# Layer norm and root mean square norms with sums by chunk and a diagonal matrix for the scaling

## The chip, the core and the metric
The kernel runs on one core of a Trainium2 chip. The metric is the device time of one execution in microseconds (us); a lower time is better. TensorE (PE) multiplies, VectorE (DVE), ScalarE (ACT) and GpSimd (POOL) work on tiles of 128 partitions, and SyncE (SP) issues the weight loads.

## What is computed
A transformer block with mixture of experts, followed by two further layers and a final norm, on 256 tokens of width 2048, all in float32:

```
x = _layer_norm(ALPHA * x + mix, ln1_w, ln1_b)
moe = _hier_moe(x, ...)                       # 32 experts, D_EXPERT 512
ple = sigmoid(x @ w_pg) * (p @ w_ple)
x = _layer_norm(ALPHA * x + moe + ple, ln2_w, ln2_b)      # "last layer norm"

def rmsnorm(x, g):                            # EPS = 1e-6
    return x * rsqrt(mean(x * x, -1) + EPS) * g

# even layer: chunked attention and an S5 state space model
x = x + concat(o_a, o_b) @ w_out_even,   inputs from rmsnorm(x, norm_even_g) @ w_in_even
# odd layer: forgetting attention, 16 heads of 128
x = x + o @ w_out_odd,                   inputs from rmsnorm(x, norm_odd_g) @ w_in_odd
return rmsnorm(x, final_norm_g)
```

The change is about the second layer norm and the three calls of rmsnorm.

## The kernel before
The whole program is written out by hand, one instruction stream for each engine, with semaphores between them. The 256 tokens are two row blocks b of 128 partitions, so x is a tile [128, 2, 2048] in SBUF. Each engine's helper issues an instruction and makes it wait for the one before it on its engine (`ordered`); so nearly all instructions of an engine carry one of a few helper lines: L137 is a PE product, L143 a PE transpose, L254 and L256 an ACT activation without and with a bias tile, L283 DVE tensor_tensor, L288 and L290 tensor_scalar, L294 scalar_tensor_tensor, L298 a reduction, L306 and L310 the statistics of a batch norm and their aggregation, L275 a reciprocal.

PSUM is a ring of four banks of 1024 columns (`Ring`, `take`, `free`). The weights come through a stream of six raw buffers; in the fp32r parts (the odd layer, the output projections) ACT copies a piece to its high half and DVE subtracts for the low half. `ahead_of(key)` does these halvings up to two pieces ahead of where PE is. In the even layer's input products the weights are used as plain float32, without halving. The experts' weights are streamed by SP (`quarter`) through ten slots of 1 MB, each reused when the product that read it is done (`used.w`).

The stretches that matter here, in the order of the program:

- **End of the experts.** PE scatters the last expert's result back to the tokens in four groups of products (row block b, column set c); DVE adds each to x (`scattered`, L1738 ff.). Then every engine branches over a rarely needed part (`beyond`) and the engines meet (`meet(7)`, `meet(8)`).
- **Second layer norm** (`layer_norm("l2", None)`). For each row block DVE takes statistics of four chunks, aggregates, adds 1e-5; ACT takes the square root; DVE the reciprocal, a subtract-and-multiply over 2048 columns, a product with ln2_w and a sum with ln2_b. Both vectors are loaded by POOL after `meet(7)`, spread over all partitions.
- **Norm of the even layer** (`rms("r1", ...)`). For each row block DVE squares (2048 columns), reduces, scales; ACT square root; DVE reciprocal and one scalar_tensor_tensor that multiplies x by the reciprocal and by the norm's weights into hne. Then PE transposes hne in four banks of eight 128x128 blocks, and ACT and DVE copy two banks each to hTe, in which channels lie on partitions. Products of the even layer start when all of hTe is there. On DVE the S5 setup follows, on POOL the tables of phases made from it.
- **Between even and odd layer.** `add_scaled("ev.out", 1.0)` adds the output product to x chunk by chunk as PE finishes each of four; then `meet(12)`, `rms("r2", ...)`, with norm_odd_g loaded by POOL after the meeting; PE transposes; ACT copies each bank to the high half of hT_ and DVE subtracts for the low half. The odd layer begins with the forget gate's rows (`od.f`).
- **End.** `add_scaled("od.out", 1.0)`, `meet(14)`, `rms("r3", ...)`, and ACT sends the result [256, 2048] with one transfer.

## Time and profile before

| | us |
|---|---|
| median of three runs | 3428.41 (3428.26 to 3434.42) |
| the profiled execution's own time | 3427.37 |
| its span in the profile | 3425.7 |
| PE busy | 3067.3 (90%) |
| DVE busy | 1568.2 (46%) |
| ACT busy | 826.3 (24%) |
| POOL busy | 266.5 (8%) |

### The profile page before, as it was taken

How to read it: one execution, taken by the hardware profiler on the slowest of the kernel's cores; microseconds unless marked ns; L12 is line 12 of the kernel's file. 1: busy time of each engine (PE TensorE's matmuls, PEld its weight loads, DVE VectorE, ACT ScalarE, POOL GpSimd, SP SyncE). 2: the span in 40 equal slices, each digit the busy share in tenths (PEclk: the TensorE clock that was granted, in tenths of full speed). 3: DMA queues.
4: the chain of work that ended last, by engine and by line, in shares of the span. 5: the costliest groups of instructions: out<-in, count | busy, mean ns of one | idle time of the engine just before them, and what ended most of it. 6: DMA issues, size and time to landing. Idle time of an engine off the chain costs nothing.

```text
span 3425.7 us, 42547 instructions
## 1 busy us (share of the span) xinstructions
PE 3067.3 (90%) x18244; PEld 2201.7 (64%) x18244; DVE 1568.2 (46%) x1856; ACT 826.3 (24%) x911; POOL 266.5 (8%) x247
## 2 busy tenths in 40 slices
PE   8978999889995899999999999679998788999987
PEld 6767777889975653333333333268777678987875
DVE  4454543564544622222222222439885445444544
ACT  3342222434431321111100110000001333443332
POOL 2042111000000000000000000044320000000000
PEclk9999988889996899999999999889999999998898
DMA  6543211336563569999999999733443365885443
GB/s 210 149 134 100 76 57 57 99 107 186 176 199 97 170 241 425 425 425 425 425 425 425 425 425 425 301 111 111 123 123 109 113 180 130 181 182 123 97 137 129
DMA packets 213809, 724.18 MB, mean 211 GB/s; under 512 B 16074, under 2 KB 18506, under 8 KB 162540
## 3 DMA queue, kind: packets, MB, share of 16 engines
q1 hardware_dynamic: 209340, 698.03, 58.7%
q0 software_dynamic: 3728, 19.15, 1.6%
q8 instruction: 146, 2.39, 0.3%
q10 hardware_dynamic: 544, 4.19, 0.3%
q14 instruction: 51, 0.42, 0.0%
HBM read 719.21 MB, written 2.10 MB: 211 GB/s over the span
## 4 chain that ended last, share of the span: by engine, by line
PE 68%; DMA 14%; DVE 12%; ACT 3%; issue 1%; POOL 1%; DVEq 0%; ACTq 0%; POOLq 0%
PE psum L137 67%; DMA t<-in_w_up 13%; DVE t L283 9%; ACT t L254 3%; PE psum L143 1%; DVE t L294 1%; DVE t L298 1%; DMA t<-in_ln_b 0%; ACT t L256 0%; POOL t L328 0%; POOL t L323 0%; DMA t<-in_r_k 0%; DMA t<-in_norm_odd_g 0%; DVE t L288 0%; DVE t L306 0%
## 5 line engine op out<-in xcount | busy, mean ns | idle before, releaser
L137 PE MATMUL psum<-t,t 128*128 128x256 f32 (+8 forms) x17134 | 2955.1, 382 | 216.1 <-DVE t L283 121.9
L137 PEld LDWEIGHTS psum<-t,t 128*128 128x128 f32 (+5 forms) x17134 | 2096.5, 178 | 1041.8 <-issue 607.8
L283 DVE TENSOR_TENSOR t<-t,t 128x1024 fp32r<-128x1024 f32 (+6 forms) x650 | 801.4, 1233 | 631.4 <-ACT t L254 595.7
L254 ACT ACTIVATE t<-t 128x1024 fp32r<-128x1024 f32 (+5 forms) x523 | 528.7, 1011 | 1036.9 <-PE psum L137 705.6
L283 DVE TENSOR_TENSOR t<-t,psum 128x1024 f32<-128x1024 f32 (+3 forms) x265 | 246.3, 929 | 760.0 <-PE psum L137 484.1
L254 ACT ACTIVATE t<-psum 128x1024 f32<-128x1024 f32 (+5 forms) x276 | 211.7, 767 | 1454.7 <-PE psum L137 1327.6
L328 POOL TENSOR_TENSOR t<-t,t 128x1024 f32<-128x1024 f32 (+9 forms) x125 | 210.3, 1682 | 572.0 <-DVE t L283 258.2
L143 PE MATMUL psum<-t,t 128*128 128x128 f32 (+1 forms) x598 | 96.9, 309 | 107.2 <-DVE t L294 62.8
L283 DVE TENSOR_TENSOR t<-psum,t 128x1024 f32<-128x1024 f32 (+5 forms) x129 | 105.1, 815 | 144.7 <-PE psum L137 125.8
L143 PEld LDWEIGHTS psum<-t,t 128*128 128x128 f32 (+1 forms) x598 | 77.5, 159 | 142.7 <-issue 89.2
L269 DVE COPY t<-psum 128x256 f32<-128x256 f32 (+5 forms) x85 | 50.4, 593 | 150.5 <-PE psum L143 97.3
L83 POOL DMA_DIRECT2D t<-in_ln_w x2 | 1.1, 554 | 1214.8 <-DVE t L283 1121.6
L298 DVE TENSOR_REDUCE t<-t 128x4 f32<-128x1024 f32 (+8 forms) x67 | 61.6, 919 | 3.0 <-ACT t L256 0.7
L254 ACT ACT_TABLE_LOAD x35 | 44.9, 1283 | 44.5 <-DVE t L290 21.5
L137 PE MATMUL psum<-t 64*64 64x64 f32 (+2 forms) x512 | 41.6, 282 | 10.3 <-ACT t L254 5.8
L302 DVE TENSOR_TENSOR_SCAN t<-t,t 128x256 f32<-128x256 f32 (+1 forms) x65 | 44.7, 688 | 2.2
L83 POOL DMA_DIRECT2D t<-in_final_norm_g x1 | 0.6, 569 | 552.7 <-DVE t L294 552.7
L137 PEld LDWEIGHTS psum<-t 64*64 64x64 f32 (+2 forms) x512 | 34.0, 184 | 14.2 <-ACT t L254 7.6
L290 DVE TENSOR_SCALAR t<-t,t,t 128x64 f32<-128x64 f32 x128 | 40.2, 314 | 4.6
L283 DVE TENSOR_TENSOR t<-t 128x2048 f32<-128x2048 f32 (+8 forms) x46 | 35.6, 773 | 1.6
L256 ACT ACTIVATE t<-psum,t 128x256 f32<-128x256 f32 (+1 forms) x56 | 24.9, 444 | 24.0 <-PE psum L137 22.4
L269 DVE COPY t<-t 64x64 f32<-64x64 f32 x64 | 29.2, 456 | 2.2
(65 smaller groups left out, 225.5 us busy)
## 6 DMA issues: line engine op xcount, KB each, us to landing
t<-in_w_gate SPq DMA_DIRECT2D x128, 1024.0 KB, 17.0
t<-in_w_up SPq DMA_DIRECT2D x128, 1024.0 KB, 19.0
t<-in_w_down SPq DMA_DIRECT2D x128, 1024.0 KB, 18.0
t<-in_w_in SPq DMA_DIRECT2D x160, 512.0 KB, 3.6
t<-in_w_in_odd SPq DMA_DIRECT2D x128, 512.0 KB, 5.5
t<-in_w_in_even SPq DMA_DIRECT2D x96, 512.0 KB, 3.8
t<-in_w_out SPq DMA_DIRECT2D x32, 512.0 KB, 3.7
t<-in_w_pg SPq DMA_DIRECT2D x32, 512.0 KB, 4.4
```

The costliest lines, as they stand in the source:

```text
L83: self.e.dma_start(out, in_).then_inc(self.counts.sem(name), 16)
L137: ins = self.e.matmul(o, l, r, start=start, stop=stop, skip_group_check=True)
L143: ins = self.e.transpose(o, i, self.ident[0:k, 0:k])
L254: self.put(self.e.activation(o, i, f, scale=scale), event)
L256: self.put(self.e.activation(o, i, f, bias=bias, scale=scale), event)
L269: self.put(self.e.tensor_copy(o, i), event)
L283: self.put(self.e.tensor_tensor(o, a, b, op), event)
L290: self.put(self.e.tensor_scalar(o, a, s1, s2, o1, o2), event)
L294: self.put(self.e.scalar_tensor_tensor(out=o, in0=a, scalar=s, in1=b, op0=o1, op1=o2), event)
L298: self.put(self.e.tensor_reduce(o, i, AX.X, op), event)
L302: self.put(self.e.tensor_tensor_scan(o, d0, d1, init, o0, o1), event)
L328: self.put(self.e.tensor_tensor(o, a, b, op), event)
```

## The change
The second layer norm and the three root mean square norms are rewritten:

- **Sums chunk by chunk.** Where DVE adds a chunk to x (the last expert's scatter, the even and the odd output product), it takes the batch norm statistics of that chunk at once. The mean square is the variance plus the squared mean. Squares and reductions over 2048 columns are gone.
- **Layer norm 2 and norm r1 in one pass** (`second_norm`): for each 512 columns two scalar_tensor_tensor, `(x - mean) * ln2_w` and `x * inv + ln2_b`, and new statistics. ln2_w and ln2_b are loaded through SP's expert slots, behind the last expert's weights.
- **Scaling as a product.** The reciprocal of each token goes on the diagonal of a 128x128 matrix (`diag[b]`, the identity times a column), and a float32 product of each block of x with it replaces both the scaling and the transpose. The weights of the norm (`gains`) now lie along partitions and are applied when the bank is read: in the even layer by 24 ACT activations of 128 columns with a scale tile and a bias tile (a column of zeros) and one DVE operation of 1024 columns, in the odd layer by 16 ACT activations (high half) and 16 scalar_tensor_tensor on DVE (low half), each of 256 columns.
- **Four parts.** The last norm is scaled by chunks of 512 columns and ACT sends each of four parts when both row blocks are there.
- The meetings 8, 9, 12, 13 and 14 are gone, some tiles have other places, and POOL's selector for the odd layer and the load of final_norm_g wait for earlier events.

```diff
@@ def vector_program
+            def second_norm():
+                aggregate()
+                v.ts(spread, var, 1e-5, None, ALU.add, event=("l2.var",))
+                v.wait_ge(("l2.std",))
+                v.rcp(inv, stdev)
+                first = place["w_down", 31, 3] + 1
+                v.wait_ge(("landed.w", first), ("landed.w", first + 1))
+                for b in range(2):
+                    for ci in range(4):
+                        xc, cs = x[:, b, 512 * ci:512 * ci + 512], slice(512 * ci, 512 * ci + 512)
+                        v.stt(xc, xc, mv[:, b, 0:1], l2w[:, cs], ALU.subtract, ALU.mult)
+                        v.stt(xc, xc, inv[:, b:b + 1], l2b[:, cs], ALU.mult, ALU.add)
+                        sums(v, 0, ci, b, 512 * ci)
+                    v.bn_aggr(m2, lst[:, 0:24])
...
+                    v.ts(s2, s2, 1e-6, None, ALU.add, event=("r1.var", b))
+                    v.wait_ge(("r1.std", b))
+                    v.rcp(i2, d2)
+                    v.ts(diag[b], ident, i2, None, ALU.mult, event=("r1.diag", b))
@@ def scattered
+                            if ex == 31:
+                                for h in range(2):
+                                    sums(v, 24 * b, 2 * c + h, b, 1024 * h + 512 * c)
@@ def tensor_program
-            turn_into("ev.T", hne, 2048, ("ev.h",))
+            for b in range(2):
+                for h in range(2):
+                    ps = pe.take("ev.T", b, h)
+                    pe.wait_ge(("r1.diag", b))
+                    for k in range(8):
+                        pe.mm(ps[:, 128 * k:128 * k + 128], x[:, b, 1024 * h + 128 * k:1024 * h + 128 * k + 128], diag[b],
+                              True, True, event=("ev.T", b, h) if k == 7 else None)
@@ def scalar_program
-            for j in (0, 2):
-                a.wait_ge(("ev.T", j))
-                a.copy(hTe[:, 4 * j:4 * j + 4, :].rearrange("p k (b t) -> p b k t", b=2),
-                       a.bank("ev.T", j).rearrange("p (b k t) -> p b k t", b=2, k=4), event=("ev.hT", "act"))
+            std("l2", lst[:, 54:56], lst[:, 52:54])
+            for b in range(2):
+                std("r1", lst[:, 61:62], lst[:, 60:61], b)
+                for h in range(b, 2):
+                    a.wait_ge(("ev.T", b, h), ("landed.gains",))
+                    for k in range(8):
+                        a.activation(hTe[:, 8 * h + k, 128 * b:128 * b + 128],
+                                     a.bank("ev.T", b, h)[:, 128 * k:128 * k + 128], ACT.Identity, bias=cols[:, 2:3],
+                                     scale=gains[0][:, 8 * h + k:8 * h + k + 1], event=("ev.hT", "act"))
...
-            a.load(("landed.out",), [(out[0].rearrange("(b p) d -> p b d", p=128), hn)])
+            for ci in range(4):
+                cs = slice(512 * ci, 512 * ci + 512)
+                a.wait_ge(("out.h", ci))
+                a.load(("landed.out", ci), [(whole[:, :, cs], hn[:, :, cs])])
@@ def pool_program
-            g.load(("landed.l2",), [(lnw, along("ln2_w")), (lnb, along("ln2_b"))])
-            g.load(("landed.r1",), [(rwe, along("norm_even_g_2"))])
```

How it moves instructions. On DVE, behind the last expert's sums, before (t_76 is x, t_72 the small sums, t_113 and t_114 ln2, t_175 hne; from the second row block's statistics on):

```order
L306 BN_STATS t_72<-t_76 128x6 x4
L310 BN_AGGR t_72<-t_72 128x2
L288 TENSOR_SCALAR t_72<-t_72 128x1
L275 RECIPROCAL t_72<-t_72 128x1
L290 TENSOR_SCALAR t_76<-t_76,t_72 128x2048
L283 TENSOR_TENSOR t_76<-t_76,t_113 128x2048
L283 TENSOR_TENSOR t_76<-t_76,t_114 128x2048
L283 TENSOR_TENSOR t_175<-t_76 128x2048
L298 TENSOR_REDUCE t_177<-t_175 128x1
L290 TENSOR_SCALAR t_177<-t_177 128x1
L275 RECIPROCAL t_177<-t_177 128x1
L294 SCALAR_TENSOR_TENSOR t_175<-t_76,t_177,t_176 128x2048
```

and now (t_134 and t_135 are ln2, t_61 the identity, t_62 the diagonal of row block 0; "..." stands for three more chunks):

```order
L306 BN_STATS t_72<-t_76 128x6 x8
L2150 UNCONDITIONAL_BRANCH
L310 BN_AGGR t_72<-t_72 128x2 x2
L288 TENSOR_SCALAR t_72<-t_72 128x2
L275 RECIPROCAL t_72<-t_72 128x2
L294 SCALAR_TENSOR_TENSOR t_76<-t_76,t_72,t_134 128x512
L294 SCALAR_TENSOR_TENSOR t_76<-t_76,t_72,t_135 128x512
L306 BN_STATS t_72<-t_76 128x6
...
L294 SCALAR_TENSOR_TENSOR t_72<-t_72 128x1
L288 TENSOR_SCALAR t_72<-t_72 128x1
L275 RECIPROCAL t_72<-t_72 128x1
L288 TENSOR_SCALAR t_62<-t_61,t_72 128x128
```

The statistics stand ahead of the branch, the norm's scaling over 2048 columns is gone, and a small diagonal ends each row block. On ACT at the same place, before (t_72 and t_177 the square roots, t_168 hTe, the copies of whole banks):

```order
L2485 UNCONDITIONAL_BRANCH
L254 ACT_TABLE_LOAD
L254 ACTIVATE t_72<-t_72 128x1 x2
L254 ACTIVATE t_177<-t_177 128x1 x2
L254 ACTIVATE t_168<-psum 128x2x4x128 x2
L254 ACT_TABLE_LOAD
L254 ACTIVATE t_204<-t_203 128x32
```

and now (t_167 is hTe, t_111 the gains, t_70 the column of zeros):

```order
L2548 UNCONDITIONAL_BRANCH
L254 ACT_TABLE_LOAD
L254 ACTIVATE t_72<-t_72 128x2
L254 ACTIVATE t_72<-t_72 128x1
L256 ACTIVATE t_167<-psum,t_70,t_111 128x128 x16
L254 ACTIVATE t_72<-t_72 128x1
L256 ACTIVATE t_167<-psum,t_70,t_111 128x128 x8
L254 ACT_TABLE_LOAD
L254 ACTIVATE t_184<-t_183 128x32
```

The second row block's square root now stands behind the 16 reads of the first block. On DVE between the even and the odd layer, before (t_165 is the scaled x, t_78 and t_77 the low and high half):

```order
L294 SCALAR_TENSOR_TENSOR t_76<-t_76,psum 128x2x512
L283 TENSOR_TENSOR t_165<-t_76 128x2048
L298 TENSOR_REDUCE t_167<-t_165 128x1
L290 TENSOR_SCALAR t_167<-t_167 128x1
L275 RECIPROCAL t_167<-t_167 128x1
L294 SCALAR_TENSOR_TENSOR t_165<-t_76,t_167,t_166 128x2048
L283 TENSOR_TENSOR t_165<-t_76 128x2048
L298 TENSOR_REDUCE t_167<-t_165 128x1
L290 TENSOR_SCALAR t_167<-t_167 128x1
L275 RECIPROCAL t_167<-t_167 128x1
L294 SCALAR_TENSOR_TENSOR t_165<-t_76,t_167,t_166 128x2048
L283 TENSOR_TENSOR t_78<-psum,t_77 128x2x4x128 x4
```

and now (t_62 and t_63 are the diagonals):

```order
L283 TENSOR_TENSOR t_76<-t_76,psum 128x2x512
L306 BN_STATS t_72<-t_76 128x6 x2
L310 BN_AGGR t_72<-t_72 128x2 x2
L283 TENSOR_TENSOR t_72<-t_72 128x2 x2
L288 TENSOR_SCALAR t_72<-t_72 128x2
L275 RECIPROCAL t_72<-t_72 128x2
L288 TENSOR_SCALAR t_62<-t_61,t_72 128x128
L288 TENSOR_SCALAR t_63<-t_61,t_72 128x128
L294 SCALAR_TENSOR_TENSOR t_78<-psum,t_112,t_77 128x256 x16
```

Ten operations of the norm, six of them over 2048 columns, became ten small ones, and the four low halves of 1024 columns became 16 of 256.

## Rows read from the trace of the kernel before

**Rows 1.** Chain of waits, two joints: start us, us, engine and tile, count.
```profile
2243.84 6.42 PE psum L143 x32
2251.63 55.49 PE psum L137 x256
...
2836.27 3.66 PE psum L143 x16
2844.95 5.64 PE psum L137 x48
```

**Rows 2.** Timeline of DVE at the three joints; in brackets idle before, and releaser.
```profile
2197.96 5.20 DVE L283 TENSOR_TENSOR t<-t,psum 128x1024 f32<-128x1024 f32 x4 [7.93 <-PE psum L137]
2206.20 2.88 DVE L306 BATCH_NORM_STATS2 t<-t 128x6 f32<-128x512 f32 x4 [3.04 <-issue]
...
2211.27 0.16 DVE L275 RECIPROCAL t<-t 128x1 f32<-128x1 f32 x1 [1.71 <-ACT t L254]
...
2815.62 1.22 DVE L294 SCALAR_TENSOR_TENSOR t<-t,psum 128x1024 f32<-128x1024 f32 x1 [0.46 <-PE psum L137]
...
3400.84 1.22 DVE L294 SCALAR_TENSOR_TENSOR t<-t,psum 128x1024 f32<-128x1024 f32 x1 [6.00 <-PE psum L137]
```

**Rows 3.** Groups of ACT by form: line, shapes, count | busy us, mean ns | idle.
```profile
L254 ACT ACTIVATE t<-psum 128x256 f32<-128x256 f32 x80 | 30.7, 384 | 145.0 <-PE psum L137 140.0 <-PE psum L143 0.7
...
L256 ACT ACTIVATE t<-psum,t 128x256 f32<-128x256 f32 x40 | 19.0, 475 | 16.0 <-PE psum L137 14.9
...
L256 ACT ACTIVATE t<-psum,t 128x128 f32<-128x128 f32 x16 | 5.9, 368 | 8.0 <-PE psum L137 7.5
L256 ACT ACTIVATE t<-t,t 128x256 f32<-128x256 f32 x8 | 4.8, 600 | 0.3
```

**Rows 4.** Timeline of PE in the mLSTM part; two records are one float32 product.
```profile
661.07 0.47 PE L137 MATMUL psum<-t 128*128 128x128 f32 x2
661.37 0.28 PE L137 MATMUL psum<-t,t 128*128 128x1 f32 x2
...
664.24 0.77 PE L137 MATMUL psum<-t 128*128 128x128 f32 x2
664.81 0.42 PE L137 MATMUL psum<-t,t 128*128 128x1 f32 x2
```

**Rows 5.** Groups of DVE by form, columns as in rows 3.
```profile
L294 DVE SCALAR_TENSOR_TENSOR t<-t,t,t 128x2048 f32<-128x2048 f32 x6 | 14.1, 2352 | 0.2
...
L306 DVE BATCH_NORM_STATS2 t<-t 128x6 f32<-128x512 f32 x16 | 11.1, 694 | 3.6 <-issue 3.0
...
L294 DVE SCALAR_TENSOR_TENSOR t<-t,t,t 128x255 f32<-128x255 f32 x8 | 3.9, 484 | 0.3
...
L294 DVE SCALAR_TENSOR_TENSOR t<-t,t,psum 128x256 f32<-128x256 f32 x8 | 3.8, 480 | 26.5 <-PE psum L137 26.5
```

**Rows 6.** Stretches: us, PE, PEld, DVE, ACT, POOL busy, clock, DMA, GB/s.
```profile
2816.00:2822.00 6.00, 0.00 (x0) 0.00 (x0) 5.57 (x4) 0.17 (x1) 0.58 (x1) 0.79 1.01 160
2838.00:2840.00 2.00, 2.00 (x11) 2.00 (x11) 0.70 (x1) 1.07 (x2) 0.00 (x0) 0.51 0.00 0
2840.00:2842.00 2.00, 1.75 (x16) 1.52 (x14) 1.52 (x2) 1.91 (x2) 0.00 (x0) 1.00 0.00 0
2842.00:2845.00 3.00, 0.05 (x1) 0.06 (x2) 2.68 (x3) 1.19 (x3) 0.00 (x0) 1.00 0.00 0
3130.00:3135.00 5.00, 5.00 (x13) 2.59 (x11) 0.67 (x2) 0.00 (x0) 0.00 (x0) 0.50 0.01 3
3308.00:3312.00 4.00, 3.32 (x8) 2.64 (x9) 1.85 (x2) 0.52 (x1) 0.00 (x0) 0.50 0.18 55
```

**Rows 7.** ACT's output issue, in its timeline.
```profile
3418.91 0.40 ACTq L83 DMA_DIRECT2D out<-t  x1
```

**Rows 8.** DMA issues: KB each, median us to landing.
```profile
t<-in_w_out_odd SPq DMA_DIRECT2D x32, 512.0 KB, 3.6
...
out<-t ACTq DMA_DIRECT2D x1, 2048.0 KB, 6.3
```

More of the change, by code:

```diff
@@ L444, in build @@
         bg = alloc(32)
+        gains = [at(invm_at + 768 + 16 * k, 16) for k in range(2)]
+        diag = [shiftd, carry]
         assert top[0] <= invm_at + 896
@@ new lines, in add_and_sum @@
+            def add_and_sum(key):
+                for ci in range(4):
+                    v.ahead_of(key, ci)
+                    cs = slice(512 * ci, 512 * ci + 512)
+                    v.wait_ge((key, ci))
+                    v.tt(x[:, :, cs], x[:, :, cs], half(v.bank(key, ci)), ALU.add)
+                    v.free(key, ci)
+                    for b in range(2):
+                        sums(v, 24 * b, ci, b, 512 * ci)
+            mv = lst[:, 48:52].rearrange("p (b k) -> p b k", b=2)
+            mean, var = mv[:, :, 0], mv[:, :, 1]
@@ L2117, in vector_program @@
[L2117 to L2122 removed]
+            root_mean_square("r2")
+            for b in range(2):
+                v.ts(diag[b], ident, inv[:, b:b + 1], None, ALU.mult, event=("r2.diag", b))
+            for j in range(4):
+                v.ahead_of("od.T", j)
+                ps = v.bank("od.T", j).rearrange("p (b k t) -> p b k t", b=2, k=4)
+                dh, dl = [z[:, 4 * j:4 * j + 4, :].rearrange("p k (b t) -> p b k t", b=2) for z in hT_]
+                v.wait_ge(("od.Th", j))
+                for k in range(4):
+                    v.stt(dl[:, :, k, :], ps[:, :, k, :], gains[1][:, 4 * j + k:4 * j + k + 1],
+                          dh[:, :, k, :].bitcast(F32), ALU.mult, ALU.subtract, event=("od.hT",))
+                v.free("od.T", j)
@@ L2125, in scalar_program @@
+            odd()
+            add_and_sum("od.out")
+            root_mean_square("r3")
+            v.wait_ge(("landed.r3",))
+            for ci in range(4):
+                cs = slice(512 * ci, 512 * ci + 512)
+                for b in range(2):
+                    v.stt(hn[:, b, cs], x[:, b, cs], inv[:, b:b + 1], rwt[:, cs], ALU.mult, ALU.mult,
+                          event=("out.h", ci) if b else None)
         def scalar_program(e):
```

140 lines of the change are left out of this document (67 added, 73 removed).

## The prediction

> **What bounds the kernel now.** I read the chain of waits first, then the timelines of the engines at its joints, then the clock by stretch. The program is TensorE (PE) work end to end, except at three joints where one x must be complete before anything goes on. At the first, the last expert's sums end on VectorE (DVE) at 2203.16 [rows 2]; PE stands still until 2243.84, then transposes for 6.42 us and starts the even layer at 2251.63 [rows 1]. At the second, between the even and the odd layer, the last product's sum ends at 2816.84 [rows 2], transposes start at 2836.27 and the odd layer at 2844.95 [rows 1]. At the third, x is complete at 3402.06 [rows 2] and the span ends at 3425.7: 6.8 us after the single output transfer is issued at 3418.91 [rows 7]. Between the joints PE is the chain, so a gain at a joint is handed on whole unless something else is late there. I lay out the changed joints instruction by instruction and subtract.
>
> **Prices.** DVE: statistics of 128x512 0.694, with the 0.03 to the next 0.72. The three-operand scaling of 512 columns lies on the line between 0.484 (255 columns) and 2.352 (2048): 0.484 + 257 x 0.00104 = 0.75, 0.785 with its gap [rows 5]. From the end of the variance to the instruction after the reciprocal: 1.71 idle (the square-root table is loaded in it) + 0.16 + 0.04 = 1.9 [rows 2]; with the table in place, 0.47. ScalarE (ACT): a PSUM read of 128x256 is 0.384 plain and 0.475 with a bias from a tile, so an operand from a tile costs 0.09; the new reads have two, so 0.566 for 256 columns and 0.368 + 0.09 = 0.46 for 128; pitches 0.60 and 0.49. Bounds: the one-operand rows, and 0.60 + 0.03 of the two-operand form from SBUF [rows 3]. PE: no row has these products alone; the nearest is a float32 product of 128 columns in the mLSTM part: 0.30 from start to start at full clock (661.07 to 661.37), 0.57 at half (664.24 to 664.81) [rows 4]. A bank of eight is 2.4 or 4.6. Half of 0.57 could be hidden at best, for the transposes it replaces take 0.23 at the low clock (16 in 3.66) [rows 1].
>
> **First joint.** Eight statistics go in between the four last sums: 2197.96 + 4 x 1.30 + 8 x 0.72 = 2208.95. Queued behind them are the weight loads of the even layer and the S5 loads on the POOL queue, 6 us later than before; nothing wants them before 2245, and three transfers of 1 MB have left that queue. The two ln2 rows ride on the SP queue behind the last experts, when DVE is 30 us from wanting them: free. The 3.04 us of issue time after the branch stay [rows 2]: 2212.0. Two aggregations and one small operation 0.77, square root and reciprocal 1.9: 2214.65. Per row block b: 4 x (2 x 0.785 + 0.72) = 9.17, aggregation and two small ones 0.73, reciprocal 0.47, diagonal 0.26: 10.6. So diagonal 0 is there at 2225.25, variance 1 at 2235.15. PE has been idle and is at half clock: bank (0,0) ends at 2229.8, (0,1) at 2232.2. ACT drains each with eight reads, 3.9 us: 2233.8 and 2237.7. Here a **new wait** appears: the square root for block 1 stands behind these 16 reads on ACT, so it comes at 2237.9 and not at 2235.3, and diagonal 1 at 2238.45. PE: 4.6 + 2.4 gives 2245.4; ACT's last eight reads end at 2249.4. The even layer starts there, against 2251.63: **2.2** earned of 8 us that DVE gains. DVE's own half (one 1.22 us operation) and the S5 setup behind it are done in that cover; the setup starts 2 to 4 us earlier as well, since its memsets no longer come after the last copy, so POOL's phase tables stay ahead.
>
> **Clock at the restart.** PE then has stood for 4.0 us. The granted clock after work that ended at 2815.56 had fallen within the stretch to 2822 (mean 0.79, so some 2.5 of its 6 us at half); the odd output projection, after a pause, began at half clock (0.50 over 3308 to 3312); but after 3.19 us from 2841.76 it was still 1.00 [rows 6]. From a cold start it is back after about 4 us (transposes from 2836.27, 0.51 up to 2840, 1.00 after) [rows 1, 6]. I take cold: half of 4 us, **2.0** lost. First joint net 0.2.
>
> **Second joint.** Sum ends 2816.84; two statistics 1.45 (the six others run while PE still multiplies: DVE has over 9 of 22 us free per chunk), aggregations 0.58, three small 0.56, square root and reciprocal 1.9, two diagonals 0.52: 2821.9. The 2816.88 to 2836.12 of squares, reductions, a load of norm_odd_g and scalings are gone. PE cold again: first bank 2826.5, the others by 2833.7. ACT is the slow one: 16 reads x 0.60 = 9.5, to 2836.05; the last four low halves on DVE (0.480 + 0.03 each [rows 5]) to 2838.2. The odd layer starts 6.6 us earlier; its restart after 4.6 us of standing costs 2.0: net **4.6**. The forget-gate rows and the split weights behind it keep their order.
>
> **Third joint.** Sum 3402.06, two statistics, aggregations, three small, 1.9: 3406.6. Eight scalings x 0.785: 3412.9. The last quarter, 512 KB, takes 3.6 like a load of 512 KB, not the 6.3 of the whole, and 0.5 stay behind it (3418.91 + 6.3 against the span) [rows 7, 8]: 3417.0, **8.7** earned. Bounds for the quarter: 1.6 (a quarter of 6.3) and 6.3.
>
> Sum: 0.2 + 4.6 + 8.7 = 13.5. The profiled execution took 3427.37 (span 3425.7), so 3413.9; the median of the runs, 3428.41, is 1.0 above it: **3414.9 us**.
>
> **A rule of the skill, weighed.** The window 2838 to 2840 is at 0.51 and 2840 to 2842 at 1.00 with only transposes running [rows 6]. The Trainium skill ("TensorE: Matmul & The Clock Gate", Part 4: PE-mode transpose) says that transposes do not count as PE work for the clock, so that they run low; real products would then bring the clock up where transposes did not, and the change would gain both restarts (the result of rival 1). By that rule 3410.9, by the rows 3414.9: the trace contradicts it here.
>
> **Rivals.** (1) The clock stays up over both restarts: pauses of 4.0 and 4.6 are little longer than the 3.19 that did no harm. 13.5 + 4.0 = 17.5: **3410.9**. (2) Products as slow as at half clock throughout. In the mLSTM part the clock fell during just such products, with PE busy: 0.30 apiece at 661.07, 0.57 at 664.24 [rows 4]. Then block 1 ends at 2247.6 and the even layer starts at 2251.6 (0, less 2 for the restart); od.T banks end at 2840.2, last low half at 2844.7 (0.2, less 2). Net 8.7 - 3.8 = 4.9: **3423.5**. (3) The four parts do not do what they say: a quarter takes as long as the whole, so the third joint earns 6.0: **3417.6**. (4) The drains are as cheap as one-operand reads (0.40 and 0.50), or the quarter lands in 1.6, together with (1): about **3406**. (5) **Slower.** The restarted layers stay at half clock far beyond 4 us. It happens: PE was busy in all of 3130 to 3135 at 0.50 [rows 6], some 30 us in all, in the odd layer's scores. Were the first 30 us of both restarted layers like that, 2 x 15 are lost: 17.5 - 30 = -12.5, **3440.9**. It decides from 35 us of added half clock on. Against it: the layer's first products are the same as before, and they ran at full clock from a restart within 2 us of transposes.
>
> **Chances.** Forecast 0.50; (1) 0.20; (2) 0.13; (3) 0.08; (4) 0.05; (5) 0.04. The unknown prices (reads 0.50 to 0.63 for 0.60, products, quarter) move the forecast by about 4 either way. Range 3407 to 3424: it leaves out (4), (5) and half of (2) with thin tails. A measurement here tells 0.2%, 6.9 us, from no change. Faster by more: the forecast but for a tail, (1), (3), (4): 0.81. Within: (2) and the tail: 0.15. Slower: 0.04.
>
> **What would show it.** Right: the even layer's first product some 2 us earlier with ACT's reads just before it, a reciprocal that waits on ACT for over 2 us in the second block, reads of 0.46 and 0.57, products of 0.57 then 0.30, a low clock in the first 4 us of each layer, the odd layer 4 to 7 us earlier relative to its last sum, and the end about 15 us after the last sum instead of 24. Wrong: reads above 0.63, a DVE wait for the ln2 rows, a pause on POOL's phase tables, or half clock without idle time behind it.

## The result and the profile after

The changed kernel takes 3409.79 us (median of five runs, 3405.9 to 3410.73) against 3428.26 (five runs, 3423.31 to 3434.42): ratio 0.9945, interval 0.9931 to 0.996. The forecast was 3414.9 with a range of 3407 to 3424. The profiled execution took 3409.92 us, its span is 3407.6 (3425.7 before); the mean granted clock is 0.945 (0.941).

**First joint.** Timeline of DVE of the changed kernel (start us, us, engine, line, operation, out<-in, shapes, count; in brackets idle time before, and what ended it), the rows that answer to [rows 2]:

```profile
2199.47 1.22 DVE L283 TENSOR_TENSOR t<-t,psum 128x1024 f32<-128x1024 f32 x1 [7.93 <-PE psum L137]
...
2215.68 0.56 DVE L310 BATCH_NORM_AGGREGATE t<-t 128x2 f32<-128x24 f32 x2 [5.18 <-issue]
...
2218.17 0.17 DVE L275 RECIPROCAL t<-t 128x2 f32<-128x2 f32 x1 [1.71 <-ACT t L254]
...
2241.30 0.16 DVE L275 RECIPROCAL t<-t 128x1 f32<-128x1 f32 x1 [2.19 <-ACT t L254]
```

ACT, same kernel and place:

```profile
2233.09 7.88 ACT L256 ACTIVATE t<-psum,t,t 128x128 f32<-128x128 f32 x16 [4.46 <-PE psum L137]
...
2247.51 3.90 ACT L256 ACTIVATE t<-psum,t,t 128x128 f32<-128x128 f32 x8 [6.25 <-PE psum L137]
```

and PE (two records are one float32 product):

```profile
2229.30 6.71 PE L137 MATMUL psum<-t,t 128*128 128x128 f32 x32 [24.64 <-DVE t L288]
2241.84 5.63 PE L137 MATMUL psum<-t,t 128*128 128x128 f32 x32 [5.83 <-DVE t L288]
2251.46 4.76 PE L137 MATMUL psum<-t,t 128*128 128x256 f32 x13 [3.99 <-ACT t L256]
```

The new wait is there: the second row block's square root stands behind 16 reads on ACT, ends at 2241.26, and DVE's reciprocal has waited 2.19 for it. A read takes 0.49 and a product 0.42 (6.71 for 16; PE was at half clock for 6 of these 6.7 us). PE starts the even layer after 3.99 us of standing, on ACT's last reads. The issue time after the branch is 5.18, not the 3.04 of [rows 2].

**Clock at the restarts.** Stretches of the changed kernel (us, busy time of PE, PE weight loads, DVE, ACT, POOL, granted clock, DMA share, GB/s), answering to [rows 6]. In both joints PE runs at half clock for 3.5 to 5 us once it has restarted:

```profile
2252.00:2254.00 2.00, 2.00 (x7) 1.68 (x6) 0.60 (x4) 1.66 (x4) 0.00 (x0) 0.61 0.00 0
...
2256.00:2258.00 2.00, 2.00 (x11) 1.75 (x10) 1.32 (x7) 0.42 (x2) 0.00 (x0) 1.00 0.08 7
...
2838.00:2840.00 2.00, 1.78 (x9) 1.25 (x10) 1.29 (x2) 0.52 (x1) 0.00 (x0) 0.50 0.00 0
...
2842.00:2844.00 2.00, 2.00 (x16) 1.50 (x14) 0.00 (x0) 0.00 (x0) 0.00 (x0) 0.76 0.66 136
```

Its chain of waits, answering to [rows 1]: the even layer's first 256 records take 57.21 us instead of 55.49, and the forget gate's rows (od.f) 7.85 instead of 5.64.

```profile
2251.46 57.21 PE psum L137 x256
...
2838.22 7.85 PE psum L137 x48
```

**Second joint.** DVE and ACT of the changed kernel, in order of time:

```profile
2816.07 1.28 ACT L254 ACT_TABLE_LOAD   x1
2817.66 1.22 DVE L283 TENSOR_TENSOR t<-t,psum 128x1024 f32<-128x1024 f32 x1 [0.41 <-PE psum L137]
...
2821.80 0.17 DVE L275 RECIPROCAL t<-t 128x2 f32<-128x2 f32 x1 [0.27 <-ACT t L254]
...
2826.28 9.71 ACT L256 ACTIVATE t<-psum,t,t 128x256 fp32r<-128x256 f32 x16 [4.51 <-PE psum L137]
...
2836.03 2.04 DVE L294 SCALAR_TENSOR_TENSOR t<-psum,t,t 128x256 fp32r<-128x256 f32 x4 [0.41 <-ACT t L256]
```

The reciprocal has waited 0.27, not the 1.71 that the prediction charged: ACT loaded the square-root table at 2816.07, before the last sum had even begun. ACT's 16 reads (9.71, 0.607 each) are the bound of the stretch, and DVE's last four low halves end it.

In the kernel before, this joint had a wait of its own that the change removes with the load. DVE there:

```profile
2825.92 0.16 DVE L275 RECIPROCAL t<-t 128x1 f32<-128x1 f32 x1 [4.24 <-DMA t<-in_norm_odd_g]
```

The first row block's reciprocal waited 4.24 us for norm_odd_g (3.86 in a second profile), where the square root alone, done at 2823.32, would have cost 1.71. So some 2.5 us of that joint were a load that came late. The kernel before with this load alone moved ahead was not run.

**Third joint.** The same, up to the end of the span at 3407.6; below it the row of DMA issues (KB each, median us to landing) that answers to [rows 8]:

```profile
3393.43 1.22 DVE L283 TENSOR_TENSOR t<-t,psum 128x1024 f32<-128x1024 f32 x1 [6.00 <-PE psum L137]
...
3397.57 0.17 DVE L275 RECIPROCAL t<-t 128x2 f32<-128x2 f32 x1 [0.27 <-ACT t L254]
3398.20 6.26 DVE L294 SCALAR_TENSOR_TENSOR t<-t,t,t 128x512 f32<-128x512 f32 x8 [0.47 <-DVE t L275]
3399.77 5.10 ACTq L83 DMA_DIRECT2D out<-t  x4
```

```profile
out<-t ACTq DMA_DIRECT2D x4, 512.0 KB, 2.7
```

**The whole span in stretches.** For every profile of this study (one execution each), from its trace: start of the first of the last expert's four sums; J1 (first joint) from there to the start of the first stretch of 160 records in the even layer's chain (2322.30 before); even, from there to the start of the last ev.out sum; J2 (second joint) to od.q, the product after od.f (2856.73 before); odd, to the start of the last od.out sum; J3 (third joint) to the end of the span. The kernels below the first four are the experiments of the next section.

| kernel | first sum | J1 | even | J2 | odd | J3 | J1+J2+J3 |
|---|---|---|---|---|---|---|---|
| before | 2197.96 | 124.34 | 493.32 | 41.11 | 544.11 | 24.86 | 190.3 |
| before_again | 2194.88 | 125.19 | 494.37 | 42.71 | 544.14 | 24.81 | 192.7 |
| after | 2199.47 | 123.79 | 494.40 | 34.55 | 541.22 | 14.17 | 172.5 |
| after_again | 2200.89 | 124.77 | 492.62 | 34.66 | 541.45 | 14.21 | 173.6 |
| meets_back | 2200.33 | 123.27 | 493.80 | 36.28 | 535.38 | 15.64 | 175.2 |
| undo_j1 | 2197.69 | 125.74 | 494.94 | 34.36 | 544.54 | 13.83 | 173.9 |
| one_output | 2200.95 | 123.36 | 494.27 | 34.98 | 539.82 | 17.82 | 176.2 |
| warm | 2195.66 | 122.96 | 492.55 | 34.59 | 535.39 | 14.15 | 171.7 |
| root_first | 2197.24 | 122.02 | 493.99 | 35.24 | 540.19 | 14.22 | 171.5 |
| stats_late | 2198.56 | 121.96 | 494.05 | 35.18 | 539.95 | 13.80 | 170.9 |
| odd_tr | 2197.60 | 122.99 | 493.81 | 29.47 | 542.23 | 13.80 | 166.3 |
| even_tr | 2197.44 | 119.85 | 494.16 | 34.63 | 544.81 | 14.11 | 168.6 |
| combo | 2196.03 | 118.66 | 493.33 | 27.91 | 538.77 | 14.10 | 160.7 |
| combo2 | 2199.19 | 117.32 | 493.10 | 27.90 | 543.98 | 14.11 | 159.3 |

Between the first two profiles, 18.1 us are gone: -1.5 ahead of the joints, 0.55 at J1, -1.1 in the even layer, 6.6 at J2, 2.9 in the odd layer, 10.7 at J3. The joints alone gave 18.4 (mean of two profiles each, 191.5 and 173.1), and the medians of the runs differ by 18.5. That they agree to 0.1 us is luck, since the interval of the ratio leaves 14 to 24 us; that the joints carry the gain is read from the traces.

### The profile page after: what moved, and what is told of

Its sections match the earlier page's. It is cut to its first block, busy times and chain, and to the rows that moved or that the text cites. A ratio compares the mean times of both kernels' runs of the same rounds, so it can differ in the third digit from the quotient of the medians.

```text
span 3407.6 us, 42738 instructions
## 1 busy us (share of the span) xinstructions
PE 3081.0 (90%) x18308; PEld 2215.1 (65%) x18308; DVE 1553.6 (46%) x1901; ACT 839.7 (25%) x942; POOL 264.6 (8%) x245
## 4 chain that ended last, share of the span: by engine, by line
PE 69%; DMA 13%; DVE 11%; ACT 4%; issue 1%; POOL 1%; DVEq 0%; ACTq 0%; POOLq 0%
PE psum L137 68%; DMA t<-in_w_up 13%; DVE t L283 8%; ACT t L254 3%; DVE t L294 1%; ACT t L256 1%; PE psum L143 1%; DVE t L298 1%; DVE t L306 0%; POOL t L328 0%; POOL t L323 0%; DMA t<-in_r_k 0%; DVE t L288 0%; DMA t<-in_ln_b 0%; DMA t<-in_b_re 0%
## 5 line engine op out<-in xcount | busy, mean ns | idle before, releaser
L137 PEld LDWEIGHTS psum<-t,t 128*128 128x128 f32 (+5 forms) x17262 | 2120.1, 178 | 1085.5 <-issue 628.6
L283 DVE TENSOR_TENSOR t<-t,t 128x1024 fp32r<-128x1024 f32 (+7 forms) x646 | 790.4, 1224 | 621.0 <-ACT t L254 585.3
L283 DVE TENSOR_TENSOR t<-t,psum 128x1024 f32<-128x1024 f32 (+3 forms) x273 | 256.1, 938 | 770.3 <-PE psum L137 494.5
L143 PE MATMUL psum<-t,t 128*128 128x128 f32 (+1 forms) x534 | 86.3, 305 | 43.8 <-DVE t L283 27.9
L143 PEld LDWEIGHTS psum<-t,t 128*128 128x128 f32 (+1 forms) x534 | 67.3, 156 | 78.1 <-DVE t L283 35.1
L298 DVE TENSOR_REDUCE t<-t 128x4 f32<-128x512 f32 (+8 forms) x61 | 47.9, 785 | 2.8 <-ACT t L256 0.7
L294 DVE SCALAR_TENSOR_TENSOR t<-t,t,t 128x512 f32<-128x512 f32 (+3 forms) x48 | 29.6, 618 | 2.2 <-DVE t L275 0.5
```

Source lines behind the costliest of these rows:

```text
L137: ins = self.e.matmul(o, l, r, start=start, stop=stop, skip_group_check=True)
L143: ins = self.e.transpose(o, i, self.ident[0:k, 0:k])
L283: self.put(self.e.tensor_tensor(o, a, b, op), event)
L294: self.put(self.e.scalar_tensor_tensor(out=o, in0=a, scalar=s, in1=b, op0=o1, op1=o2), event)
L298: self.put(self.e.tensor_reduce(o, i, AX.X, op), event)
```

## The experiments

Each was made from the changed kernel, but for before_again. A time is the median of its runs, a ratio is to runs of the kernel before made beside them. Effects of one to three microseconds can't be read from ratios whose intervals reach some 6 us to either side; they are read from the joints of the trace.

### What differs from one execution to the next
Both kernels once more, without an edit.

> The kernel before, profiled a second time, to see what differs from one execution to the next. Theory (the half clock stretches inside the odd layer's scores fall differently from one execution to the next, and the 3.0 us that the changed kernel gains there are chance): the time between the start of od.q and the start of od.out differs by 1 us or more between the two profiles of this same kernel. Rival (the stretches are fixed by the work that the kernel gives to TensorE): the same 5 us windows are at half clock and that time agrees within 0.5 us. The joints themselves, DVE's 1.71 us before the reciprocal and 3.04 us after the branch, agree within 0.1 us by both.

> The changed kernel, profiled a second time. Theory (DVE's 5.18 us after the branch belong to this kernel's code): 5.2 again within 0.3, and 3.0 in the other kernel. Rival (chance of one execution): another value between 3 and 5. The odd layer from od.q to od.out, 3.0 us shorter than before in the first profile: by chance theory it moves by over 1 us, by the rival it comes out the same within 0.5 us. Second joint 34.5 us from last sum to od.q, third 14.2 from last sum to the end of the span.

The kernel before took 3427.81 us, the changed one 3410.87. The odd layer from od.q to the product od.out: 451.95 and 451.97 in the two profiles of the kernel before, so the theory on record for before_again (1 us or more apart) missed; 448.96 and 450.00 in those of the changed one, but 444.5, 452.3, 449.0, 444.5 in meets_back, undo_j1, one_output and warm, whose code is the same there. So it is not fixed by the work. The mean granted clock over this stretch goes with it: 0.96 where it took 444.5, 0.94 where it took 452. The 2.9 us that the first pair showed there are not credited to the change, but that stays open: the other twelve profiles of the table average 540.6 for the odd layer, and both of the kernel before have 544.1. The issue time after the branch is 3.04 and 2.82 in the kernel before (0.1 had been allowed), 5.18 and 4.98 in the changed one: it belongs to the code. Two more things were not as in the first profile. The wait for ln2_b was 1.03 there and is 2.90 now:

```profile
2212.41 4.62 DVE L283 TENSOR_TENSOR t<-t,t 128x2048 f32<-128x2048 f32 x2 [2.90 <-DMA t<-in_ln_b]
```

And od.f, 5.64 before, took 7.24 in the same kernel, at half clock, after a pause of 2.57 us, where in the first profile the clock had stayed up over 3.19. Stretches of before_again:

```profile
2842.00:2844.00 2.00, 0.23 (x2) 0.21 (x3) 1.61 (x2) 0.51 (x2) 0.00 (x0) 0.97 0.00 0
2844.00:2846.00 2.00, 2.00 (x11) 1.34 (x10) 1.11 (x1) 1.92 (x2) 1.73 (x2) 0.50 0.01 0
```

### The table load and the meetings

```diff
             add_and_sum("ev.out")
+            v.meet(12)
             add_and_sum("od.out")
+            v.meet(14)
```
(and the same for PE and ACT; POOL has no part in these two meetings, though the expectation speaks of all four engines)

> The changed kernel with all four engines meeting again before the square roots of the second and the third joint (the former meetings 12 and 14); nothing else differs. Theory (a meeting holds back ACT's load of the square-root table; without it the load runs while DVE still takes statistics): the idle time before both reciprocals goes from 0.27 back to 1.71, the load starts after the last sum and not 1.6 us before it, each joint is 1.4 us longer, the time 3412.7. Rival (the load is early because its root now takes both row blocks in one operation, or because DVE's small operations give it time): idle stays at 0.3, joints and time unchanged, 3409.8.

3411.85 us, ratio 0.9955 (0.9938 to 0.9973). ACT and DVE of meets_back at the second joint, then DVE at the third:

```profile
2821.70 1.28 ACT L254 ACT_TABLE_LOAD   x1 [5.97 <-DVE t L288]
...
2823.23 0.17 DVE L275 RECIPROCAL t<-t 128x2 f32<-128x2 f32 x1 [1.96 <-ACT t L254]
...
3394.61 0.17 DVE L275 RECIPROCAL t<-t 128x2 f32<-128x2 f32 x1 [1.68 <-ACT t L254]
```

The load stands behind the last small operation again, the waits are 1.96 and 1.68, J2 is 1.6 and J3 1.45 longer than in the changed kernel. The effect is shown in both places: without the meeting the load runs early, with it it doesn't. The rival, one root for both row blocks, falls, since that is unchanged here. The median can't show 3 us.

How the meeting does it is shown only in part. If it merely held ACT until the others had arrived, the load would start when they had. In the kernel before DVE arrives at the last meeting with its last sum, at 3402.06, and POOL, past the same meeting, issues its load at 3402.61; but on DVE and ACT there stand

```profile
3406.82 0.15 DVE L290 TENSOR_SCALAR t<-t 128x1 f32<-128x1 f32 x1
3407.15 1.28 ACT L254 ACT_TABLE_LOAD   x1 [13.56 <-DVE t L290]
```

ACT's table load starts 5 us after the meeting, behind the variance that is the root's input. In meets_back too it starts 0.44 and 0.16 us behind the variance. So behind a meeting the load waits for the root's input as well; why is open.

### The first joint as before

```diff
-            second_norm()
+            layer_norm("l2", None)
+            rms("r1", ("ev.h",), hne, rse, rwe)
-                        pe.mm(ps[...], x[...], diag[b], True, True, ...)
+            turn_into("ev.T", hne, 2048, ("ev.h",))
```
(with the loads and the meetings 8 and 9)

> The changed kernel with the first joint as before: second layer norm and norm r1 over 2048 columns, the ln2 rows and norm_even_g loaded by POOL, transposes, four copies of whole banks, meetings 8 and 9; second and third joint stay changed. Theory (the first joint nets nothing: 1.7 us earlier start, 1.7 us of cold clock): time the same as the changed kernel's within 1 us, 3409.8; from the first scatter sum to the end of the even layer's first stretch of products 111.4 in both; idle after the branch back at 3.04. Rival A (the first joint's change earns, hidden by chance in one profile): 2 us or more above, 3412. Rival B (the idle time after the branch is longer for a reason that lies elsewhere in the code): 5.2 again.

3411.22 us, ratio 0.995 (0.9933 to 0.9967), next to 0.9945 for the whole change: the first joint's part can't be told from nothing. In the trace J1 is 125.74, 1 to 2 us longer than in the two profiles of the changed kernel. Rival A is not excluded at that size, and its source is seen: DVE waits 3.78 us for ln2_b here. Waiting for the transfer that the change sends through the SP queue cost 1.0, 2.9 and 3.8 us in three profiles. Rival B falls: 2.74 after the branch.

### Four parts or one

```diff
-            for ci in range(4):
-                a.wait_ge(("out.h", ci))
-                a.load(("landed.out", ci), [(whole[:, :, cs], hn[:, :, cs])])
+            a.wait_ge(("out.h", 3))
+            a.load(("landed.out", 3), [(whole, hn)])
```

> The changed kernel with the result sent by one transfer of 2048 KB after the eighth scaling, in place of four of 512 KB; the eight scalings stay. Theory (the four parts earn by leaving only 512 KB behind the last scaling, which land in 2.7 us and not in 6.3): from the last sum to the end of the span 14.2 becomes 17.8, time 3413.4. Rival (the last part waits in the queue behind the three before it, or the whole is faster when it is alone): the end moves by less than 1 us.

3413.73 us, ratio 0.995 (0.9932 to 0.9968); J3 is 17.82, as the theory says to a tenth. Its one transfer of 2048 KB takes 6.3 to landing, as in [rows 8].

So 3.65 us of the third joint's 10.7 come from the parts. Of the other 7, 1.45 are the table load (meets_back); the rest, from the sums by chunk and one root for both row blocks, is what remains and was not tested by itself.

### Extra products in the pauses

```diff
+            ps = pe.take("ev.warm")
+            for k in range(10):
+                pe.mm(ps[:, 0:128], x[:, 1, 0:128], diag[1], True, True, ...)
             even()
```
(and 18 ahead of odd())

> The changed kernel with extra float32 products of 128 columns on TensorE, written to a PSUM bank that nobody reads, during the pauses in which the banks are drained: 10 after the last ev.T bank, 18 after the last od.T bank. Nothing waits for them but the next layer's products behind them on TensorE. Theory (the first 4 us of each layer run at half clock because TensorE has stood still for 4 to 6 us; work in the pause keeps the clock up): granted clock 1.00 in the first 2 us of both layers, the first stretch of the even layer back from 57.2 to 55.5, od.f from 7.9 to 5.6: 3.9 us earned, time 3406. If the extra products outlast the drains, part of it is paid back, at most 1 us. Rival (the clock falls for another reason, such as what the layer's first products draw): the first 4 us stay at 0.5 to 0.6 and the time is the same or up to 1 us more.

3404.43 us, ratio 0.9928 (0.991 to 0.9946). Chain of waits and stretches of warm:

```profile
2247.31 55.52 PE psum L137 x256
...
2832.37 7.25 PE psum L137 x48
```

```profile
2248.00:2250.00 2.00, 2.00 (x11) 1.75 (x10) 0.74 (x4) 1.65 (x4) 0.00 (x0) 1.00 0.00 0
...
2832.00:2834.00 2.00, 1.63 (x8) 1.16 (x9) 1.45 (x2) 0.68 (x1) 0.00 (x0) 0.61 0.00 0
2834.00:2836.00 2.00, 2.00 (x12) 1.43 (x10) 0.00 (x0) 0.00 (x0) 0.00 (x0) 0.54 0.72 113
```

Half of the theory holds. At the even layer the clock stays up and 1.7 us come back. At the odd layer PE had worked from 2816.17 to 2830.45, at full clock from 2824, and stood for 1.92 us; the clock fell all the same. Nor is the even layer's 1.7 handed on whole: J1 is 122.96 against 123.0 to 124.8 in five profiles with the same first joint. Before the even layer's stretch of 160 records PE waits for four 64x64 copies on DVE that run beside POOL's operations; they took 2.40 in the changed kernel and 3.59 in warm, which gives 1.2 of it back. Why they take longer is open. The median is lower than the trace accounts for: 1 to 2 us at the joints; the odd layer's 535.39 was at the low end of its spread.

### The square root behind the reads

```diff
-                std("r1", ..., b)
+                if b == 0: std("r1", ..., b)
                 ...
                     for k in range(8):
+                        if (b, h, k) == (0, 1, 4): std("r1", ..., 1)
```

> The changed kernel with one instruction of ACT moved: the square root of the second row block's norm r1 stands behind 12 of the first block's 16 reads and not behind all. Theory (the reciprocal waits 2.2 us for a root that is queued behind reads): its idle time falls from 2.19 to about 0.5, the second block's products start 1.7 us earlier, and the even layer 1.5 us earlier, since the four reads that now come after the root are done while DVE makes the diagonal; time 3408.5. Rival (ACT is the bound in this stretch, and what the root gains the reads lose): the idle time falls but the even layer starts within 0.3 us of where it did.

3406.35 us, ratio 0.993 (0.9913 to 0.9946). DVE of root_first:

```profile
2236.70 0.16 DVE L275 RECIPROCAL t<-t 128x1 f32<-128x1 f32 x1 [0.27 <-ACT t L254]
```

From the first aggregation to the even layer's start 34.47, against 36.08 (mean of seven profiles whose root is behind all 16 reads, 35.7 to 36.8). 1.6 earned, as the theory says (1.5): the wait was on the path.

### The statistics and the branch

```diff
-                            if ex == 31: sums(...)        # between the last expert's sums
             def second_norm():
+                for b in range(2):
+                    for ci in range(4):
+                        sums(v, 24 * b, ci, b, 512 * ci)
                 aggregate()
```

> The changed kernel with the eight statistics of the first joint taken behind the branch and not between the last expert's sums, as before the change. Theory (the time without a row after the branch is DVE's fetch of the code that it jumps to, and it runs while DVE's short operations ahead of the branch do not cover it; with 5.2 us of sums directly ahead of the branch it was 2.7 to 3.0, with statistics ahead of it 4.8 to 5.2): it comes back to 3.0, and from the first scatter sum to the first aggregation it takes 5.2 + 3.0 + 5.8 = 14.0 against 16.2 now, so the statistics ahead of the branch have lost 2.2 us and not gained 3.2. Rival (the gap is longer for another reason, such as what lies behind the branch in this kernel): it stays at 5.0, and the stretch takes 16.0.

3407.79 us, ratio 0.9933 (0.9917 to 0.995). DVE of stats_late:

```profile
2198.56 5.20 DVE L283 TENSOR_TENSOR t<-t,psum 128x1024 f32<-128x1024 f32 x4 [7.93 <-PE psum L137]
2206.53 5.79 DVE L306 BATCH_NORM_STATS2 t<-t 128x6 f32<-128x512 f32 x8 [2.77 <-issue]
2212.36 0.56 DVE L310 BATCH_NORM_AGGREGATE t<-t 128x2 f32<-128x24 f32 x2
```

13.80 from the first sum to the first aggregation, against 15.2 to 16.2 in the eight profiles with the statistics ahead of the branch. So it is the place of the statistics that makes the gap: 2.74 to 3.04 in the six profiles with only sums ahead of the branch, 4.2 to 5.2 with statistics in between. Why, the trace does not show; that DVE fetches the code behind the branch in that time was only argued. Taking the statistics early gains nothing at this joint: the four last sums stand one behind the other on DVE (5.20 for four), with no idle time that statistics could fill. It loses 2 us.

### Diagonal product or transposes

```diff
             for ci in range(4):
+                for b in range(2):
+                    v.stt(hn2[:, b, cs], x[:, b, cs], inv[:, b:b + 1], rwt[:, cs], ALU.mult, ALU.mult, ...)
...
-                        pe.mm(v[:, b, k, :], x[...], diag[b], True, True, ...)
+                        pe.tr(v[:, b, k, :], hn2[...], ...)
...
-                for k in range(4):
-                    a.activation(dh[:, :, k, :], ps[:, :, k, :], ACT.Identity, bias=cols[:, 2:3], scale=gains[1][...], ...)
+                a.copy(dh, ps, event=("od.Th", j))
```

> The changed kernel with the second joint's scaling back on DVE and its transposes back on TensorE, everything else there as changed (sums by chunk, no meetings): eight scalings of 512 columns, each pair followed by its transposes; ACT reads each bank whole for the high half, DVE for the low half; norm_odd_g is loaded early. Theory (with the product by the diagonal, ACT's sixteen reads of 0.61 bound the stretch, and the product earns less than the chunk-wise sums do): scalings end 10.6 us after the last sum begins, low halves at 15.6, and od.f starts 15.8 after it in place of 20.6: 4.8 earned, time 3405. Rival (the diagonal product is what brings the second joint its gain, since eight scalings and transposes at half clock take its place): od.f starts at 20 or later, time 3410 or more.

3402.42 us, ratio 0.992 (0.9898 to 0.9942). DVE and PE of odd_tr:

```profile
2814.40 1.22 DVE L283 TENSOR_TENSOR t<-t,psum 128x1024 f32<-128x1024 f32 x1 [0.43 <-PE psum L137]
...
2818.82 6.26 DVE L294 SCALAR_TENSOR_TENSOR t<-t,t,t 128x512 f32<-128x512 f32 x8
2825.19 5.21 DVE L283 TENSOR_TENSOR t<-psum,t 128x1024 fp32r<-128x1024 f32 x4
```

```profile
2820.42 4.40 PE L143 MATMUL psum<-t,t 128*128 128x128 f32 x24 [6.05 <-DVE t L294]
...
2830.55 11.67 PE L137 MATMUL psum<-t,t 128*16 128x256 f32 x86 [4.25 <-DVE t L283]
```

od.f starts 16.15 after the last sum began, against 20.56; J2 is 29.47 against 34.6. The diagonal product costs the second joint 5 us: what it saves on DVE (8 scalings, 6.26) comes back as 16 reads of 0.607 on ACT in place of 4 of 1.02, with DVE's low halves tied behind them. norm_odd_g is loaded ahead of the joint here, and DVE does not wait for it.

The same at the first joint:

> The changed kernel with the same done to the first joint: norm r1's scaling back on DVE, in four chunks of 512 columns for each row block, TensorE transposes each chunk, ACT copies three banks whole and DVE one; norm_even_g is loaded by POOL behind the meeting. Theory (24 reads of 0.49 on ACT, and the root behind 16 of them, cost more than eight scalings of 0.785 on DVE): the second block's root no longer waits (0.3 for 2.2), and from the first aggregation to the start of the even layer it takes 32 us where the changed kernel took 35.7 to 36.8; the cold clock after it stays or shrinks; time 3406. Rival (the diagonal product is needed here, since DVE is the bound and 6.3 us more of it are paid in full): 38 us or more, time 3412.

3407.15 us, ratio 0.9929 (0.9912 to 0.9945). The second reciprocal waits 0.27, the even layer starts 32.35 after the first aggregation (36.08 before), J1 is 119.85: 4 us earned, as the theory says. Not all of it is the product's price. The square root queued behind the 16 reads is gone as well, and root_first earned 1.6 by moving that root alone, with the product kept. Against root_first 2.1 us remain (32.35 and 34.47). Here too the product was dearer than what it replaced.

### All of it together
Both of these, the statistics behind the branch, `a.activation(lst[:, 63:64], cols[:, 2:3], ACT.Sqrt)` (a square root of a zero, for its table) ahead of ACT's meeting 7, and products of the identity on PE that nobody reads.

> All that the runs so far point to, together: both joints with scalings by chunk on DVE and transposes, the first joint's statistics behind the branch (2.0), the square-root table loaded ahead of the meeting by an extra square root of a zero (1.4), and extra float32 products of the identity, which nobody reads, on TensorE: 2 before each chunk of the second row block and 4 at the end of the first joint, 16, 2 and 4 at the second (2.0 at the first joint; 0 to 2 at the second, where such products did not keep the clock up before). Theory (the parts add): 3.7 + 4.8 + 2.0 + 1.4 + 2.0 = 13.9 below the changed kernel, 3396, with 4 either way from where the odd layer's half clock stretches fall. Rival (the parts stand in each other's way: DVE is already the bound at the first joint and the extra products delay the transposes): 3402 or more.

3392.03 us against 3431.82: ratio 0.9892 (0.9875 to 0.9908), with combo2 the fastest of this study; its slowest run (3399.23) is below the fastest of the changed kernel (3405.9). The first reciprocal waits 0.43 (1.71 in the changed kernel), the even layer's first stretch takes 55.52, od.f 5.62. J1+J2+J3 is 160.7, 12.4 below the changed kernel's 173.1, where 13.9 had been expected: the even layer starts 33.49 after the first aggregation and not 31.1. Stretches of combo there:

```profile
2238.00:2240.00 2.00, 2.00 (x12) 2.00 (x11) 1.45 (x2) 0.00 (x0) 0.00 (x0) 0.50 0.00 0
```

PE is busy without a break at half clock, with extra products between the transposes. I read this as the extra products being on the path; the last run moved them.

> As combo, with the extra products moved: 22 before the first chunk of the second row block at the first joint (while DVE takes that block's statistics and TensorE has nothing to do) and 1, not 2, before each later chunk, 3 at its end; at the second joint 24 ahead of the transposes, not 16, 2 between banks, 10 at the end, not 4. Theory (in combo the extra products stood on the path: they ran at half clock between the last transposes and cost 2.4 us of the 2.0 they gave; work ahead of the transposes brings the clock up before they start): clock 1.00 from the second block's transposes on, from the first aggregation to the start of the even layer 31.1 in place of 33.5, with its first stretch still at 55.5; od.f 16.1 after the last sum as in combo, where DVE is the bound, at full clock; time 3389.6. Rival (the clock is at half again by the time the transposes start, or the 22 products stay at half clock and run past 2236): 33.5 or more, time 3392 or more.

3394.12 us, ratio 0.9902 (0.9885 to 0.9919), not to be told from combo by the median. It came out between theory and rival: 32.28. PE of combo2, and its stretches:

```profile
2229.27 5.56 PE L137 MATMUL psum<-t 128*128 128x128 f32 x44
2239.27 1.12 PE L143 MATMUL psum<-t,t 128*128 128x128 f32 x4 [4.45 <-DVE t L294]
```

```profile
2232.00:2234.00 2.00, 2.00 (x21) 2.00 (x20) 1.93 (x3) 0.00 (x0) 0.00 (x0) 1.00 0.00 0
...
2240.00:2242.00 2.00, 2.00 (x11) 2.00 (x10) 1.80 (x4) 0.00 (x0) 0.00 (x0) 0.50 0.00 0
```

The 22 products brought the clock up, but after 4.45 us of standing it was at half again. At the second joint PE was at 1.00 throughout, and the odd layer started no earlier (J2 27.90 and 27.91; od.f 16.15 after the last sum, as in odd_tr without any extra product): DVE's eight scalings and four low halves are the bound there. What the extra products give at the second joint is od.f in 5.62 and not 7.18 (odd_tr).

## Why the prediction was right, point by point

- **The form of the sum was right.** The gain lies at the three joints and is handed on: 18.4 at the joints in the traces. It was 5 us larger than forecast. The larger errors are times of the new kernel that were priced too high, at the second and third joint; at the first, two errors nearly cancelled.
- **First joint, forecast 0.2, measured 0.4 to 1.1** (J1 means 124.8 and, over five profiles, 123.6). Start 2.2 earlier: 1.7 and 1.8 (51.99 and 52.80 from the first sum, against 53.67 and 54.59). Restart -2.0: -1.7 and -2.8 (57.21 and 58.28 against 55.49). These two would give 0 and -1.0; what stands between the even layer's first records and its stretch of 160 came out 0.6 and 1.4 shorter, which the prediction did not have. The wait behind ACT's reads came where it was said, reads at their price (0.49). Two errors nearly cancelled: the 3.04 after the branch did not stay 3.04 (5.18; stats_late shows that the statistics ahead of the branch do it; -2.1), and the second block's products took 5.63 (6.71 in the second profile) and not 7.0, since they cost 0.42 at half clock, not 0.57, and in the first profile the clock came up in them (0.84 over 2245 to 2247). The 0.57 had been read from [rows 4], from the start of such a product to the start of a product of another shape.
- **Second joint, forecast 4.6, measured 6.6** (8.1 by the second pair). The term that was off is "square root and reciprocal 1.9": it carried the 1.71 of idle time over, while without the meeting the table load runs ahead (1.71 became 0.27, 1.44 less; meets_back gives it back). The first bank was there after 3.6 us and not 4.6. The price of the cold restart was right against the first profile (7.85 and 7.31 against 5.64), but that the kernel before paid nothing there was luck of that profile; in the second it paid 1.6 of it too. Two slips in the sum: 16 x 0.60 is 9.6 and not 9.5, and 2844.95 - 2838.2 is 6.75 and not 6.6.
- **Third joint, forecast 8.7, measured 10.7.** Again 1.44 for the table, and the quarter landed in 2.7, not 3.6 (0.9): I had taken a load's duration for a store's. Against it 0.47 of idle ahead of the scalings that had not been counted. 8.7 + 1.44 + 0.9 - 0.47 = 10.6.
- **Rival 1** (the clock stays up) is refuted in all profiles of the changed kernel, and the argument for it, length of the pause, with it: the clock stayed up over 2.43 us (combo) and 3.19, and fell over 1.92 and 2.57. **Rival 2** came about in part only: in the changed kernel the first 16 products of the first joint ran at half clock for 6 of their 6.7 us, and in after_again the second 16 did throughout (0.50 up to 2249), but at 0.42 apiece and not 0.57, and at the second joint those after 2826 ran at full clock. **Rival 3**: refuted by one_output. **Rival 4**: its quarter came about in part, not its reads (0.49, 0.607). **Rival 5** did not come about: in the first profile the layers were back at full clock by 2256 and 2844.
- **Transposes and the clock.** Stretches of odd_tr, where only transposes run from 2820.42:

```profile
2820.00:2822.00 2.00, 1.58 (x8) 1.58 (x9) 1.89 (x4) 0.00 (x0) 0.00 (x0) 0.50 0.24 73
...
2824.00:2826.00 2.00, 1.59 (x15) 1.38 (x14) 1.86 (x3) 1.91 (x2) 0.00 (x0) 1.00 0.00 0
```

The clock is at half at first and at 1.00 from 2824 on, 3.6 us after they begin; in the changed kernel it took the products from 2822.67 to 2826, and at its first joint 6 us of them. So the product in place of the transposes bought no clock. The Trainium skill ("TensorE: Matmul & The Clock Gate", Part 4: PE-mode transpose) says that transposes do not count as PE work for the clock; these stretches contradict it.
- **What the prediction did not ask** is whether the diagonal product is worth having. It weighed change against before, and there the sums by chunk, the missing meetings and the four parts pay for it. odd_tr shows that it takes back 5 us at the second joint, even_tr and root_first that it takes back 2.1 at the first, with 1.6 more for the root behind its reads. The other thing it did not ask is what an earlier load of norm_odd_g would give the kernel before by itself: by its trace up to 2.5 us, not tested.

## What to carry to other kernels

Move work off the engine that bounds a joint only after costing the engine that takes it over: a per-partition gain applied on the read of a bank turns one read of 1024 columns (1.02 us) into four (2.43) or eight (3.9). At a joint, look what each small operation stands behind on its own engine: a square root moved ahead of the last four of 16 reads gave 1.6 us, a meeting removed gave 1.4 of hidden table load, twice. And profile the kernel before twice: the clock (od.f 5.64 and 7.24) and a DMA wait (1.03 and 2.90) differed by 1.6 and 1.9 us at these very joints between two executions.

## What the runs showed of the hardware that I had not expected

- Where no meeting stood ahead of it, the load of ACT's function table (1.28 us) ran as soon as ACT's instructions ahead of it were done, without waiting for the input of the activation that needs it (2816.07, variance at 2821.53). Behind a meeting it started 0.16 to 0.44 us after that input (before, changed kernel at the first joint, meets_back), even where the others had met 5 us earlier.
- The time without a row after DVE's branch depends on what DVE did ahead of it: 2.7 to 3.0 after four additions of 1.22 us, 4.2 to 5.2 with eight statistics of 0.69 between them. The cause is open.
- Whether PE restarts at half clock is not told by the length of its pause: at half after 1.92 us (warm) and 2.57 (before_again), at full after 2.43 (combo) and 3.19 (before). Work at full clock ahead of the pause did not decide either (warm). What does is open.
- In profiles with the same code the odd layer took 535.4 to 544.8 us, and the mean granted clock over it was higher where it was shorter (0.96 and 0.94 from od.q to od.out). That is the largest difference between the traces outside the joints, and larger than most effects studied here; its cause is open.
- A store of 512 KB by ACT's queue landed in 2.7 us, where a load of w_out_odd of that size by SP's took 3.6 and a store of 2048 KB 6.3 (medians).
